# A named table set ahead of ScalarE's norms: seven loads by hand in a fused two-block layer kernel

## What is computed

```python
def rmsnorm(x, g):
    y = x32 * lax.rsqrt(jnp.mean(x32 * x32, axis=-1, keepdims=True) + NORM_EPS)
    return (y * g.astype(jnp.float32)).astype(x.dtype)
...
def swiglu_layer(x, norm_g, w_gate_up, w_down):
    h = rmsnorm(x, norm_g)
    g, u = jnp.split(h @ w_gate_up, 2, axis=-1)
    return x + (jax.nn.silu(g) * u) @ w_down
...
def second_block(...):
    for l in range(DEPTH):
        h = _rms_norm(x, norm_pre[l]) * (1 + scale[:, None, :]) + shift[:, None, :]
        p = h @ w_in[l]
        o_mla = _mla_branch(...)      # norms of c_q and c_kv, silu(z), a softmax
        o_rwkv = _rwkv7_branch(...)   # tanh, sigmoid, exp, a norm of each key head and of each output head
        o_gla = _gla_branch(...)      # log_sigmoid, exp(cum), silu(z), a norm of each head
        merged = (jax.nn.sigmoid(gate_a) * o_mla + jax.nn.sigmoid(gate_b) * o_rwkv
                  + jax.nn.sigmoid(gate_c) * o_gla)
        y = merged @ w_out[l]
        x = x + gate[:, None, :] * _rms_norm(y, norm_post[l])
```

## Time and profile before

| | |
|---|---|
| median of 3 runs | 2196.87 us (2191.93 to 2196.94) |
| profiled execution | 2196.02 us, span 2194.2 us |
| mean granted clock of PE | 0.965 |
| PE busy | 1997.6 us, 91% |
| DVE busy | 1350.3 us, 62% |
| ACT busy | 741.1 us, 34%, in 1038 instructions |

### The profile page before, as it was taken

The page is one execution under the profiler, slowest core; times in us unless marked ns, Lnnn a source line. Parts: engine busy times, 40 slices in busy tenths (PEclk is TensorE's granted clock), DMA queues, the critical chain, the costliest instruction groups (busy, mean ns, idle before and its releaser), DMA issues.

```text
span 2194.2 us, 41714 instructions
## 1 busy us (share of the span) xinstructions
PE 1997.6 (91%) x18103; PEld 1836.4 (84%) x18103; DVE 1350.3 (62%) x1789; ACT 741.1 (34%) x1038; POOL 25.1 (1%) x52
## 2 busy tenths in 40 slices
PE   6968899999899999989988899997999988899997
PEld 6967799998689998979867779897988876778887
DVE  6786378746837766854663439565765664428554
ACT  4642243335633333231421323244321332314234
POOL 1000000000000000000000000000000000000000
PEclk9989999999999999999998999999999999999988
DMA  7534357963327784626421125443653540135533
GB/s 188 146 86 145 105 202 243 270 184 114 90 90 260 257 242 113 173 68 163 115 78 41 37 83 154 116 134 101 172 153 106 134 115 22 28 92 146 143 97 106
DMA packets 472912, 291.43 MB, mean 133 GB/s; under 512 B 26527, under 2 KB 467332, under 8 KB 472624
## 3 DMA queue, kind: packets, MB, share of 16 engines
q1 hardware_dynamic: 464000, 260.27, 42.1%
q0 software_dynamic: 5088, 25.31, 3.0%
q10 hardware_dynamic: 3664, 3.52, 0.6%
HBM read 288.02 MB, written 1.05 MB: 132 GB/s over the span
## 4 chain that ended last, share of the span: by engine, by line
PE 70%; DVE 13%; ACT 3%; issue 2%; DMA 1%; DVEq 0%; ACTq 0%; SPq 0%
PE bank L685 34%; PE bank L1235 5%; PE bank L1237 5%; PE bank L1236 5%; PE bank L674 4%; PE bank L644 2%; PE bank L870 2%; PE bank L862 2%; DVE rounded L710 1%; PE bank L1418 1%; PE bank L1405 1%; PE bank L767 1%; DVE arena L1056 1%; DVE arena L1067 1%; DVE arena L1051 1%
## 5 line engine op out<-in xcount | busy, mean ns | idle before, releaser
L685 PE MATMUL bank<-rounded 128*128 128x256 f32 (+1 forms) x4440 | 545.5, 284 | 22.7 <-DVE rounded L710 20.2
L685 PEld LDWEIGHTS bank<-rounded 128*128 128x128 f32 (+1 forms) x4440 | 536.3, 190 | 29.3 <-DVE rounded L710 23.7
L710 DVE TENSOR_TENSOR rounded<-arena,rounded 128x1024 fp32r<-128x1024 f32 (+1 forms) x243 | 293.1, 1213 | 89.5 <-ACT rounded L699 71.4
L1235 PE MATMUL bank<-parts 128*128 128x256 f32 x1024 | 290.6, 284 | 3.7 <-DVE parts L1914 2.1
L1236 PE MATMUL bank<-parts 128*128 128x256 f32 x1024 | 289.8, 283 | 0.0
L1237 PE MATMUL bank<-parts 128*128 128x256 f32 x1024 | 289.8, 283 | 0.0
L685 PE MATMUL bank<-common,arena 128*128 128x256 f32 x1280 | 289.4, 386 | 0.0
L685 PEld LDWEIGHTS bank<-common,arena 128*128 128x128 f32 x1280 | 246.2, 193 | 41.6 <-issue 4.5
L750 ACT ACTIVATE arena<-bank 128x512 f32<-128x512 f32 x114 | 67.6, 597 | 485.3 <-PE bank L685 475.6
L1235 PEld LDWEIGHTS bank<-parts 128*128 128x128 f32 x1024 | 196.5, 192 | 4.8 <-DVE parts L1906 2.1
L1236 PEld LDWEIGHTS bank<-parts 128*128 128x128 f32 x1024 | 196.6, 192 | 0.1
(11 more groups left out here) (394 smaller groups left out, 2566.2 us busy)
## 6 DMA issues: line engine op xcount, KB each, us to landing
arena<-in_w_in SPq DMA_DIRECT2D x190, 512.0 KB, 3.8
whole<-in_ffn_w_gate_up SPq DMA_DIRECT2D x44, 1024.0 KB, 5.1
arena<-in_ada_w POOLq DMA_DIRECT2D x32, 768.0 KB, 6.2
whole<-in_ffn_w_down SPq DMA_DIRECT2D x16, 1408.0 KB, 7.2
arena<-in_rec_w_in SPq DMA_DIRECT2D x36, 512.0 KB, 3.8
arena<-in_att_w_qkv SPq DMA_DIRECT2D x24, 512.0 KB, 3.7
arena<-in_rec_w_out SPq DMA_DIRECT2D x16, 512.0 KB, 3.9
arena<-in_mla_w_o SPq DMA_DIRECT2D x16, 512.0 KB, 4.1
```

What stands on the lines that cost most here:

```text
L685: last = pe.matmul(psum[s][0:c, m % 2 * T:m % 2 * T + T], w[a][:, k, cols], x[b][:, k, :], start=(k, a, b) == (0, 0, 0), stop=k == job.kt ...
L710: dve.tensor_tensor(raw_view(job_of[u], u, UNIT_LOW), raw, high_view(job_of[u], u).bitcast(F32), ALU.subtract)\
L1235: pe.matmul(bank, w_hi, x_hi, start=start and k == 0, stop=False)
```

## The change

A helper is added that loads the table set with logarithm and exponential together, by its name, and it is called at seven places of ACT's program. Nothing else is altered: the compiler still places loads of its own where it finds that one is needed.

```diff
+        def logarithms_act():
+            act.preload_act_table_set("natural_log_exp_and_others")
...
             for j in range(UPS):
                 up_turn(j, j < UPS - 1)
+            logarithms_act()
             down_high_parts(0, 1)
...
         def take_in_act():
+            logarithms_act()
             act.dma_start(cst[:, 0:FIRST_CONST], A["const"][:, 0:FIRST_CONST]).then_inc(first_constants.sem, 16)
...
             act.wait_ge(z_done.sem, z_done.due(act))
+            logarithms_act()
             act.wait_ge(ssd_buffers_free.sem, 1)
             up_high_act(0, 0, 0)
             rms_act(512, 2)
...
             take_units(act, j["r"], keep(raw[1], ACT.Copy, 1))
+            logarithms_act()
             act.wait_ge(cumulated.sem, cumulated.due(act))
...
             for n, at in (("rz0", 0), ("rz1", 4), ("rz2", 6)):
                 take_units(act, j[n], keep(ZR[:, at:], ACT.Silu))
+            logarithms_act()
             for k in range(0, DK, 2):
...
             take_units(act, j["gz"], keep(GZ, ACT.Silu))
+            logarithms_act()
             for t in range(TT):
...
             take_units(act, j["gc"], keep(GT, ACT.Sigmoid), high_before(j["gc"], 2))
+            logarithms_act()
             high_act(j["go"].through())
```

## The result

The changed kernel takes 2179.52 us, median of 5 runs (2172.03 to 2183.13), against 2196.87 for the kernel before: a ratio of 0.9927 [0.9903, 0.9951], so 0.7% faster. The forecast was 2180.2. The profiled execution of after took 2179.52 us, with a span of 2177.7; that of before has 2194.2, a difference of 16.5 us where the sum gave 16.68.

A forecast was written before the change was run, and what follows sets the result against it. PE was taken as the bound, busy 91% of the span and holding 70% of the last-ending chain; the terms sum to -16.68 us, taking the median from 2196.87 to 2180.2 us, range 2171 to 2190.

The forecast's parts named there:

- start: Token norm at the kernel's start: two of three loads go from the path ahead of PE's first L1123, -2.58 us.
- six norms: Recurrent group norm, both FFN norms, attention norm, its first head norm, mixer layer 0's norm: Exp's bare load goes, -7.74 us.
- GLA gates, layer 0: Gated linear attention's gates, first mixer layer: loads at L3043 and L3063 go, L3063 starts at 1334.16, not 1336.08, -1.90 us.
- GLA gates, layer 1: Gated linear attention's gates, second mixer layer: DVE gains by the loads of L3043 and L3057, -2.58 us.
- key turning, two layers: GLA's L3084: the named load lands bare between gz's last eviction and the turning, +1.30 us in each layer, +2.60.
- output norm, layer 0: Loads of Ln (0.98) and Exp (1.29) go, but DVE splits a unit and waits only 1.50: -1.47 us.
- next layer's norm: Norm behind layer 0's output norm: 2.58 us of loads go, but DVE splits two units and waits 0.36: -0.34 us.
- last norm: Final norm: DVE has nothing else to do, so Ln's 0.98 and Exp's 1.29 count, -2.27 us.
- 2: Rival, chance 0.07: automatic loads are placed again ahead of Ln and Exp, 12 loads are added, 2200.8 us.
- 1: Rival, chance 0.12: gain partly eaten as weight transfers do not follow or DVE's splitting becomes the bound, 2184 to 2194 us.
- 3: Rival, chance 0.04: slower through the clock, 1.6 us per new fall, 15 more falls needed, about 2204 us.
- 4: Rival, chance 0.07: loads called covered are not, or clock falls go away; all 37 bare 2149.4 us, half way 2165.

The follow-up runs named there:

- start_behind: The changed kernel with its first named load behind ACT's DMA issues, ahead of the token norm's squares, instead of ahead of the issues: 2180.49 us, 0.9916 of before.
- load_at_exp: The changed kernel with the same set loaded once more between Ln and Exp in each of 14 norms: 2184.38 us, 0.9946 of before.
- load_at_ln: The changed kernel with the same set loaded once more ahead of Ln in each of 14 norms: 2182.28 us, 0.9926 of before.
- late_gz: The changed kernel with the named load of GLA's norm moved from behind gz to behind the key turning: 2170.05 us, 0.9871 of before.
- issues_behind: Changed kernel with GLA's named load behind the key turning, Sigmoid's set named at two more places, last five start DMA issues behind token norm's Exp: 2172.72 us.
- after_again: The changed kernel run once more, unaltered, as the baseline on its own chip: 2182.38 us, 0.9914 of before.

## Why the prediction was right

The forecast was 16.7 us less; the two medians differ by 17.35 us, the two spans by 16.5, and the line against the clock by 17.1. Step by step, each as the step in the difference between the traces of before and after:

| place | predicted | measured |
|---|---|---|
| start | -2.58 | -3.9 at L1127, -2.7 at 60 us (-3.0 in the mean of eight traces) |
| six norms | -7.74 | -1.28 at four, -1.09 at the two of the FFNs, -7.3 |
| second head norm | -0.40 | -0.67 |
| GLA gates, layer 0 | -1.90 | about -1.5 |
| GLA gates, layer 1 | -2.58 | -2.56 |
| key turning, two layers | +2.60 | +2.84 |
| output norm, layer 0 | -1.47 | -1.6 |
| next layer's norm | -0.34 | -0.46 |
| last norm | -2.27 | -2.24 |

The sum of the right column is -2.7 - 7.3 - 0.67 - 1.5 - 2.56 + 2.84 - 1.6 - 0.46 - 2.24 = -16.2, or -16.5 with the mean of the start. The rest to 16.5 is the lower clock falling on other work in the two executions, with both signs.

- **The step that failed** is "The named load is put ahead of the DMA issues, so all of them leave 1.28 later ... the squares then start where they do now". The issues left when they always had, and the squares started without a load ahead of them; start_behind puts the 1.28 back by moving the load alone. The term of -2.58 came out near the measured -2.7 only because the third load's 1.28 was given back on the lower clock; in the mean of eight traces the term is 0.4 too small. That the term fits is luck.
- **What a bare load costs**, 1.29, held at four of the six norms that were counted in full. At the norms of the two FFNs PE waited 0.83 us for DVE (at L1235 of before). With that wait gone PE has work without a gap, and it is 1.09 earlier and not 1.29: 0.2 of the load doesn't reach it, where the prediction counted it in full. The places counted at nothing (latent norms, decays, the loads behind the FFN's gates) showed no step. load_at_exp and load_at_ln show both kinds.
- **The key turning** was the right place with a price too small: 1.42 and not 1.30 in each layer, for want of the overlap with the eviction ahead. The falls of the clock behind that wait were not in the sum either, nor those that the change spares at the gates. By the counts under late_gz they nearly cancel (estimates: 2 x 7/12 x 1.69 = 2.0 us lost, 2 x 3/4 x 1.69 = 2.5 gained), which is luck too.
- **GLA layer 0** was too large by 0.4, the wait of 0.46 us that ACT now has for DVE (L2555) ahead of L3072, L3063 of before. I had it start as soon as ACT was free.
- **The rivals.** 2 is out by the count of 37 loads. 1 shows at the two places that were in the sum and, with 0.2 us each, at the two FFN norms. 3 and 4 are out as a whole: the mean clock of after's 11 runs is 0.9627, of before's 37 it is 0.9634, and no place counted as covered shows a step. Their mechanism, falls of the clock that come and go with PE's waits, seems to be at work in GLA, once each way.

## What to carry to other kernels

Count table loads by which side of a wait they stand on: one ahead of the engine's next wait is free, one between two dependent activations costs its full 1.28 us, and the same line of code can be worth 8 us or 1.6. When loads are moved by name, put each behind the last work that the next engine is waiting for, and look at the place where the named load lands, not only at those where the automatic ones go. A longer wait of PE can cost more than its own length, in falls of the clock behind it. Where runs of one kernel spread by 11 us with the clock, take a difference of 3 us from the steps between two traces and say that the times don't show it.

## What the runs showed of the hardware

- A table load named ahead of DMA issues doesn't hold them back: load from 0.94 to 2.22, first issue at 0.98, the next at 1.45.
- ACT's DMA issues do hold back its activations: the squares, or the load ahead of them, started within 0.11 us of the end of the last issue in before, after, start_behind and issues_behind (14.62 to 14.73 in after; 9.02 to 9.12 in issues_behind), with the input landed since 7.2.
- The granted clock of the same stretch of the same program differed from one execution to the next: 0.94 and 0.78 over 1384 to 1415 us. Over 1401 to 1411 PE was granted 0.50 in after_again. What decides it stays open. Behind a wait of 2.12 us at the key turning it fell in 7 of 12 cases, behind one of 0.70 in none of 10.
